# Conditioning products of a two-block kernel: four a group in groups 8 to 23 instead of two or three in each of 24

## The chip, the cores and the metric

One core of a Trainium2 chip runs the program. The metric is the device time of one execution in microseconds (us), lower is better. The engines are TensorE (PE; its weight loads are PEld), VectorE (DVE), ScalarE (ACT), GpSimd (POOL) and SyncE (SP). Each has its own instruction queue, and they wait for one another through semaphores.

## The reference

Two transformer-like blocks on a sequence of 512 with width 1024. The part that matters here is at the beginning of the first block:

```python
mod = (jax.nn.silu(c) @ w_ada[i] + b_ada[i])[:, None, :]
shift_m, scale_m, gate_m, shift_f, scale_f, gate_f = jnp.split(mod, N_MOD, axis=-1)
h = rmsnorm(x, norm_mix_w[i]) * (1.0 + scale_m) + shift_m
x = x + gate_m * hybrid_mixer(h, ...)      # begins with proj = h @ w_in, then a causal
                                           # convolution of width 4 over the xbc columns and silu
h = rmsnorm(x, norm_mlp_w[i]) * (1.0 + scale_f) + shift_f
```

`c` is one vector of 1024, `w_ada` is 1024 x 6144. Only `shift_m` and `scale_m`, a third of `mod`, are needed before the projection. The rest is needed much later: `gate_m` when the mixer's output is added, the others in the feed-forward part.

## The kernel before

**Linear layers.** All weight matrices are streamed in units of 8 x 128 rows by 128 columns (512 KB) through a ring of two buffers of each kind. SP loads a unit into `w_raw` (line 368) as soon as the split of the unit two earlier is done (semaphore `w_split`). ScalarE rounds it to `w_hi` (line 382, `split_hi`), after the load has landed and PE has finished the unit two earlier. VectorE forms `w_lo` = `w_raw` - `w_hi` (line 388, `split_lo`). PE then multiplies three times for each of the 8 k tiles, 24 products of 512 columns a unit (line 456, `products_of`).

**The first projection.** Before it, one unit computes the 32 step-size columns. Then come 24 groups of 128 columns of xbc, one unit each. For group g PE makes its 24 products; ScalarE takes the result out twice (lines 960 and 962) and makes `w_hi` of the unit two ahead. VectorE's queue has, in a Python loop that is unrolled and so sets its order: `split_lo` for the unit two ahead, the convolution `conv` (two instructions of line 1607 and one of line 1609), the group's `dt_steps`, and then a few products of `times_c`. ScalarE finishes with a silu (line 967). In `dt_steps` the step sizes are formed in groups 0, 2 and 3 (lines 1621 to 1635, ending in the semaphore `dt_done`), and `dt_decay` in groups 6 and 7. PE turns the step sizes into tokens between its groups 4 and 5 (line 1336), which waits for `dt_done`.

**Conditioning.** `mod` is formed in 12 blocks of 512 columns. For each, `times_c` on VectorE adds up 8 products of a row tile of `w_ada` with a column of silu(c): one of line 600 and seven of line 602, each waiting for the one before through `link`. Blocks 0 to 3 run before the projection. Blocks 4 to 11 run among the 24 groups of the projection, a block in three groups (2, 3 and 3 products). The tiles of `w_ada` are 2 MB each, in two buffers; POOL issues the load of block n (line 776) when block n - 2 is done. After PE's last group, `modulation` (line 1319) turns each block's sums into columns with tiny products; the last block's waits for its last product, VectorE adds the bias (lines 1651 and 1653, semaphore `mod_ready`), and PE waits for that before the chunked scan (line 1362 on).

Of the kernel before, what the change touches and what calls it, by code (L numbers as in the profile page):

```python
# [152 lines left out]
def two_block_program(nc, I, out):  # L153
    ctx = ExitStack()
    with ctx:
        sems = {}

        def sem(name):
            if name not in sems:
                sems[name] = ctx.enter_context(nc.semaphore(name))  # L160
            return sems[name]
# [223 lines left out]
        def split_lo(dve, l, t, par, j):  # L385
            slot, _ = slot_of(l, t, par, j, 2)
            dve.wait_ge(sem("w_hi_ready"), unit_of(l, t, par, j) + 3)
            dve.tensor_tensor(wlo[slot][:], wraw[slot][:], whi[slot][:].bitcast(F32), ALU.subtract).then_inc(  # L388
                sem("w_split"), 1)
# [204 lines left out]
        def times_c(dve, link, n, k0=0, k1=KD):  # L594

            u, slot, fill = (ADA_FIRST[n], n, 1) if n < 4 else (n, n % 2, n // 2)
            w, acc = wada[slot], ada_acc[u]
            if k0 == 0:
                dve.wait_ge(sem(f"ada_in{slot}"), 16 * fill)
                link(dve.tensor_scalar(acc[:], w[:, 0, :], small[:, 8:9], None, ALU.mult))  # L600
            for k in range(max(k0, 1), k1):
                ins = dve.scalar_tensor_tensor(acc[:], w[:, k, :], small[:, 8 + k:9 + k], acc[:], ALU.mult, ALU.add)  # L602
                if k < KD - 1:
                    link(ins)
                else:
                    ins.then_inc(sem("ada_acc"), 1)
# [64 lines left out]
        def lg_view(b, i):  # L671

            _, nq, nk, _ = TT[i]
            if nk <= 512:
                return two(PS[0:nq, b, 0:nk])
            return PS[0:nq, b:b + 2, 0:nk // 2]
# [14 lines left out]
        def probs_transposed(pe, i, p):  # L691

            _, nq, nk, ntile = TT[i]
            last = pe.transpose(PS[0:META, 1, 0:nq], p[0:nq, 0:META], ident[0:nq, 0:nq])
            for t in range(1, ntile):
                last = pe.transpose(PS[:, 0, (t - 1) * P:(t - 1) * P + nq], p[0:nq, META + (t - 1) * P:META + t * P],  # L696
                                    ident[0:nq, 0:nq])
            return last

        def values_product(pe, b, i, v, p):  # L700

            _, nq, _, ntile = TT[i]
            for t in range(ntile):
                rows = META if t == 0 else P
                last = pe.matmul(PS[:, b, 0:nq], v(t)[0:rows, :], p[0:rows, t, 0:nq], start=(t == 0),  # L705
                                 stop=(t == ntile - 1))
            return last
# [857 lines left out]
        def _(dve):  # L1565
            link = Link(dve, sem("dve_link"))
# [33 lines left out]
            def conv(g, t, par):  # L1600
                evacuated(dve, L["xbc"], t, par)

                dve.wait_ge(sem("conv_out"), t * 2 + par + 1)
                dve.wait_ge(sem("conv_pad"), 2)
                u, a = ub[par], ca[par]
                for k in (2, 1):
                    link(dve.scalar_tensor_tensor(a[:], u[:, 1 + k:1 + k + S], pcol("conv_w", k * NX + g), a[:],
                                                  ALU.mult, ALU.add))
                dve.scalar_tensor_tensor(a[:], u[:, 1:1 + S], pcol("conv_w", g), a[:], ALU.mult,
                                         ALU.add).then_inc(sem("conv_done"), 1)  # L1610
# [7 lines left out]
            def dt_steps(g):  # L1618
                if g == 0:
                    dve.wait_ge(sem("dt_act"), 3)  # L1620
                    dve.tensor_scalar(u, y, 1.0, None, ALU.add).then_inc(sem("dt_u"), 1)
                elif g == 2:
                    dve.wait_ge(sem("dt_act"), 4)
                    link(dve.tensor_scalar(u, u, 1.0, None, ALU.subtract))
                    link(dve.tensor_scalar(e, u, 0.0, None, ALU.is_equal))
                    link(dve.tensor_scalar(u, u, 1e-30, None, ALU.max))
                    link(dve.reciprocal(u, u))
                elif g == 3:
                    link(dve.tensor_tensor(l, l, y, ALU.mult))
                    link(dve.tensor_tensor(l, l, u, ALU.mult))  # L1630
                    link(dve.tensor_tensor(e, e, y, ALU.mult))
                    link(dve.tensor_tensor(l, l, e, ALU.add))
                    link(dve.tensor_scalar(v, v, 0.0, None, ALU.max))
                    link(dve.tensor_tensor(v, v, l, ALU.add))
                    dve.tensor_scalar(y, v, cst[:, 2:3], -1.0, ALU.mult, ALU.mult).then_inc(sem("dt_done"), 1)
                elif g == 6:
                    dve.wait_ge(sem("dt_tok"), 3)
                    dve.tensor_tensor(wdt[:], dtok[:, 3, :, :], dtok[:, 2, :, :], ALU.subtract).then_inc(
                        sem("dt_diff"), 1)
                elif g == 7:  # L1640
                    dve.wait_ge(sem("dt_tok"), 4)
                    link(dve.tensor_tensor(wdt[:], wdt[:], dtok[:, 0, :, :], ALU.mult))
            for g in range(NX):
                split_lo(dve, L["xbc"], g // 2, g % 2, 0)
                conv(g, g // 2, g % 2)
                dt_steps(g)
                n, third = 4 + g // 3, g % 3
                times_c(dve, link, n, *((0, 2), (2, 5), (5, 8))[third])

            dve.wait_ge(sem("ada_done"), 12)  # L1650
            link(dve.tensor_tensor(modc[:, 16:48], bank(7)[:, 16:48], PC[:, 16:48], ALU.add))
# [7 lines left out]
            for i in range(24):  # L1659
                if i < 16:  # L1660
                    g, c = STEPS[i]
# [329 lines left out]
```

## Time and profile before

| | us |
|---|---|
| median of 3 runs | 2889.18 |
| lowest, highest | 2887.94, 2900.04 |
| the profiled execution | 2890.59 |
| its span in the profile | 2888.6 |
| PE busy | 2583.7 (89%) |
| VectorE busy | 1539.1 (53%) |
| ScalarE busy | 1038.0 (36%) |

The busy times are of the profiled execution. The projection's 24 groups lie between about 54 and 213 us of its span, some 5% of it. Times within the span are counted from its start.

### The profile page before, as it was taken

The numbers are of one execution on the slowest core, as the hardware profiler recorded it, in microseconds if no ns is written. First come the engines' busy times: TensorE is split into PE (matmuls) and PEld (weight loads), VectorE is DVE, ScalarE is ACT, GpSimd is POOL, SyncE is SP. The second block draws the span as 40 slices with busy tenths as digits, with TensorE's granted clock in tenths as the row PEclk, the third lists the DMA queues.
The fourth block names the chain that finished last, engine by engine and source line by source line (L and its number), as shares of the span: only waits on it lengthen the run. The fifth ranks groups of instructions, "written<-read, shape, count | busy, mean of one in ns | idle before, by whom it ended". The sixth has DMA issues, their size and how long they took to land.

```text
span 2888.6 us, 41859 instructions
## 1 busy us (share of the span) xinstructions
PE 2583.7 (89%) x15307; PEld 2253.1 (78%) x15307; DVE 1539.1 (53%) x2178; ACT 1038.0 (36%) x1718; POOL 619.4 (21%) x522
## 2 busy tenths in 40 slices
PE   5898888998979999798666899999996996999998
PEld 4677766886858878697445899999995665899998
DVE  6884555424354233458555476642557556566631
ACT  5444443434333233233233333322433443333322
POOL 0000223610620102531112511222211002411110
PEclk8999999999989989888557999999996556999999
DMA  7551111332323333232000233323321000223322
GB/s 260 160 175 30 37 37 44 95 95 80 95 67 94 95 110 95 73 96 58 1 1 8 74 90 92 87 88 94 104 77 36 1 1 20 76 87 88 93 86 89
DMA packets 378054, 222.75 MB, mean 77 GB/s; under 512 B 9986, under 2 KB 368997, under 8 KB 377957
## 3 DMA queue, kind: packets, MB, share of 16 engines
q1 hardware_dynamic: 369189, 186.74, 22.9%
q0 software_dynamic: 8160, 32.53, 3.1%
q10 hardware_dynamic: 608, 2.16, 0.2%
q8 instruction: 64, 1.05, 0.2%
q14 instruction: 33, 0.27, 0.0%
HBM read 216.49 MB, written 4.78 MB: 77 GB/s over the span
## 4 chain that ended last, share of the span: by engine, by line
PE 76%; DVE 11%; issue 7%; ACT 3%; DMA 2%; POOL 2%; POOLq 0%; ACTq 0%; DVEq 0%; SPq 0%
PE PS L456 63%; PE PS L705 4%; PE PS L685 2%; DVE ada_acc L602 1%; DMA w_raw<-in_w_in_dram 1%; PE PS L687 1%; PE PS L1382 1%; DVE rstd_headB L1951 1%; PE PS L696 1%; ACT w_hi L382 1%; PE PS L1441 1%; DVE w_lo L388 1%; PE PS L1394 1%; DVE evac L1767 1%; DVE op_lo L558 1%
## 5 line engine op out<-in xcount | busy, mean ns | idle before, releaser
L388 DVE TENSOR_TENSOR w_lo<-w_raw,w_hi 128x1024 fp32r<-128x1024 f32 x360 | 494.8, 1374 | 863.1 <-ACT w_hi L382 862.7
L456 PE MATMUL PS<-op_hi,w_hi 128*128 128x264 f32 (+2 forms) x3048 | 806.5, 323 | 67.6 <-DVE op_lo L558 31.0
L456 PE MATMUL PS<-op_lo,w_hi 128*128 128x264 f32 (+2 forms) x3048 | 796.8, 320 | 0.0
L456 PE MATMUL PS<-op_hi,w_lo 128*128 128x264 f32 (+2 forms) x3048 | 793.6, 319 | 0.0
L456 PEld LDWEIGHTS PS<-op_hi,w_hi 128*128 128x128 f32 (+1 forms) x3048 | 511.7, 191 | 127.1 <-issue 39.2
L456 PEld LDWEIGHTS PS<-op_hi,w_lo 128*128 128x128 f32 (+1 forms) x3048 | 508.8, 191 | 38.4 <-issue 0.8
L456 PEld LDWEIGHTS PS<-op_lo,w_hi 128*128 128x128 f32 (+1 forms) x3048 | 509.5, 191 | 36.8 <-issue 0.9
L382 ACT ACTIVATE w_hi<-w_raw 128x1024 fp32r<-128x1024 f32 x360 | 379.1, 1053 | 219.0 <-PE PS L456 209.5
L456 PE MATMUL PS<-ff_hi,w_hi 128*128 128x264 f32 (+1 forms) x960 | 242.0, 312 | 0.0
L456 PE MATMUL PS<-ff_hi,w_lo 128*128 128x264 f32 (+1 forms) x960 | 242.0, 311 | 0.0
L456 PE MATMUL PS<-ff_lo,w_hi 128*128 128x264 f32 (+1 forms) x960 | 241.9, 311 | 0.0
L588 POOL TENSOR_TENSOR ff_u<-ff_u,rstd 128x528 f32<-128x528 f32 x88 | 100.4, 1142 | 429.5 <-ACT ff_u L1197 391.4
L1197 ACT ACTIVATE ff_u<-PS 128x528 f32<-128x528 f32 x88 | 54.0, 613 | 343.0 <-PE PS L456 313.1
L456 PEld LDWEIGHTS PS<-ff_lo,w_hi 128*128 128x128 f32 x960 | 157.0, 188 | 10.1
L456 PEld LDWEIGHTS PS<-ff_hi,w_hi 128*128 128x128 f32 x960 | 156.9, 188 | 10.0
L456 PEld LDWEIGHTS PS<-ff_hi,w_lo 128*128 128x128 f32 x960 | 156.7, 188 | 9.9
L645 POOL TENSOR_TENSOR evac<-resid,evac 128x528 f32<-128x528 f32 (+1 forms) x40 | 52.4, 1309 | 514.0 <-ACT evac L620 513.4
L705 PE MATMUL PS<-probsT,v_tokA 128*128 128x128 f32 (+2 forms) x240 | 60.1, 387 | 76.1 <-ACT probsT L1173 75.6
L705 PEld LDWEIGHTS PS<-probsT,v_tokA 128*128 128x128 f32 (+1 forms) x240 | 45.2, 257 | 103.1 <-ACT probsT L1173 93.7
L643 POOL TENSOR_TENSOR resid<-resid,evac 128x512 f32 (+1 forms) x16 | 20.9, 1306 | 301.6 <-ACT evac L620 301.6
L705 PEld LDWEIGHTS PS<-probsTB,v_tokB 128*128 128x128 f32 (+1 forms) x240 | 53.2, 301 | 35.2 <-issue 26.2
L1743 DVE TENSOR_TENSOR norm_v<-evac 128x512 f32<-128x512 f32 x32 | 22.1, 692 | 107.3 <-ACT evac L1084 107.3
(343 smaller groups left out, 3548.7 us busy)
## 6 DMA issues: line engine op xcount, KB each, us to landing
w_raw<-in_w_up_dram SPq DMA_DIRECT2D x120, 512.0 KB, 3.9
w_raw<-in_w_in_dram SPq DMA_DIRECT2D x64, 512.0 KB, 4.0
w_raw<-in_w_down_dram SPq DMA_DIRECT2D x64, 512.0 KB, 3.9
w_ada<-in_w_ada_dram POOLq DMA_DIRECT2D x12, 2048.0 KB, 10.2
w_raw<-in_w_branch_ssd_dram SPq DMA_DIRECT2D x16, 512.0 KB, 3.9
w_raw<-in_w_in_a_dram SPq DMA_DIRECT2D x16, 512.0 KB, 3.8
w_raw<-in_w_kv_b_dram SPq DMA_DIRECT2D x16, 512.0 KB, 3.8
w_raw<-in_w_down_dram SPq DMA_DIRECT2D x16, 384.0 KB, 3.4
```

Source lines behind the costliest of these rows:

```text
L382: act.activation(whi[slot][:], wraw[slot][:], ACT.Copy).then_inc(sem("w_hi_ready"), 1)
L388: dve.tensor_tensor(wlo[slot][:], wraw[slot][:], whi[slot][:].bitcast(F32), ALU.subtract).then_inc(sem("w_split"), 1)
L456: last = pe.matmul(a[0:l.cols, h, 0:cn], w[slot][:, k, 0:l.cols], x[:, kk, c0:c0 + cn], start=(j == 0 and k == 0 and w is whi and x is l.h ...
L558: dve.scalar_tensor_tensor(lo[:, k, :], R[:, k, :], gain(k), hi[:, k, :].bitcast(F32), ALU.mult, ALU.subtract).then_inc(sem("norm_ready"), 1)
L588: pool.tensor_tensor(x, x, rs[0:L[name].cols, :], ALU.mult).then_inc(sem("scaled"), 1)
L602: ins = dve.scalar_tensor_tensor(acc[:], w[:, k, :], small[:, 8 + k:9 + k], acc[:], ALU.mult, ALU.add)
L645: link(pool.tensor_tensor(e, r, e, ALU.add))
L685: return pe.matmul(PS[0:nq, b, 0:nk], q[:, q0:q0 + nq], k[:, 0:nk], start=True, stop=True)
L687: last = pe.matmul(PS[0:nq, b + a, 0:nk // 2], q[:, q0:q0 + nq], k[:, a * nk // 2:(a + 1) * nk // 2], start=True, stop=True)
L696: last = pe.transpose(PS[:, 0, (t - 1) * P:(t - 1) * P + nq], p[0:nq, META + (t - 1) * P:META + t * P], ident[0:nq, 0:nq])
L705: last = pe.matmul(PS[:, b, 0:nq], v(t)[0:rows, :], p[0:rows, t, 0:nq], start=(t == 0), stop=(t == ntile - 1))
L1197: act.activation(halves(uu[par][:, 2:2 + T]), acc_view(l, par), ACT.Copy).then_inc(sem("evacuated"), 1)
```

## The change

The 64 products of blocks 4 to 11 no longer stand in all 24 groups. Groups 0 to 7 have none. Groups 8 to 23 have four each, a block in two groups.

```diff
                 split_lo(dve, L["xbc"], g // 2, g % 2, 0)
                 conv(g, g // 2, g % 2)
                 dt_steps(g)
-                n, third = 4 + g // 3, g % 3
-                times_c(dve, link, n, *((0, 2), (2, 5), (5, 8))[third])
+                if g >= 8:
+
+                    n, half = 4 + (g - 8) // 2, (g - 8) % 2
+                    times_c(dve, link, n, 4 * half, 4 * half + 4)
```

Only VectorE's order differs. In its queue, at the step sizes of group 2 and the beginning of group 3 (`dtT` holds the step sizes, `ada_acc` the sums of a block, `w_ada` its tile), the difference reads:

```order
 L1626 TENSOR_SCALAR dtT<-dtT 32x512
 L1627 RECIPROCAL dtT<-dtT 32x512
-L602 SCALAR_TENSOR_TENSOR ada_acc_88<-w_ada_80,small,ada_acc_88 128x512 x3
 L388 TENSOR_TENSOR w_lo_56<-w_raw_52,w_hi_54 128x1024
 L1607 SCALAR_TENSOR_TENSOR conv_acc_99<-conv_in_97,param_cols,conv_acc_99 128x512 x2
```

The last three products of block 4 are gone from between the reciprocal and the split of group 3. Further on in VectorE's queue, groups 8 and 9 stood so before (the first three products close block 6, the last two open block 7):

```order
L388 TENSOR_TENSOR w_lo_57<-w_raw_53,w_hi_55 128x1024
L1607 SCALAR_TENSOR_TENSOR conv_acc_98<-conv_in_96,param_cols,conv_acc_98 128x512 x2
L1609 SCALAR_TENSOR_TENSOR conv_acc_98<-conv_in_96,param_cols,conv_acc_98 128x512
L602 SCALAR_TENSOR_TENSOR ada_acc_90<-w_ada_80,small,ada_acc_90 128x512 x3
L388 TENSOR_TENSOR w_lo_56<-w_raw_52,w_hi_54 128x1024
L1607 SCALAR_TENSOR_TENSOR conv_acc_99<-conv_in_97,param_cols,conv_acc_99 128x512 x2
L1609 SCALAR_TENSOR_TENSOR conv_acc_99<-conv_in_97,param_cols,conv_acc_99 128x512
L600 TENSOR_SCALAR ada_acc_91<-w_ada_81,small 128x512
L602 SCALAR_TENSOR_TENSOR ada_acc_91<-w_ada_81,small,ada_acc_91 128x512
```

In the changed kernel the same two groups read:

```order
L388 TENSOR_TENSOR w_lo_57<-w_raw_53,w_hi_55 128x1024
L1607 SCALAR_TENSOR_TENSOR conv_acc_98<-conv_in_96,param_cols,conv_acc_98 128x512 x2
L1609 SCALAR_TENSOR_TENSOR conv_acc_98<-conv_in_96,param_cols,conv_acc_98 128x512
L600 TENSOR_SCALAR ada_acc_88<-w_ada_80,small 128x512
L602 SCALAR_TENSOR_TENSOR ada_acc_88<-w_ada_80,small,ada_acc_88 128x512 x3
L388 TENSOR_TENSOR w_lo_56<-w_raw_52,w_hi_54 128x1024
L1607 SCALAR_TENSOR_TENSOR conv_acc_99<-conv_in_97,param_cols,conv_acc_99 128x512 x2
L1609 SCALAR_TENSOR_TENSOR conv_acc_99<-conv_in_97,param_cols,conv_acc_99 128x512
L602 SCALAR_TENSOR_TENSOR ada_acc_88<-w_ada_80,small,ada_acc_88 128x512 x4
```

Two groups now hold eight products, a whole block, and block 4 opens here instead of in group 0. The queues of PE, ScalarE, POOL and SP hold the same instructions in the same order as before; the loads of `w_ada` for blocks 6 to 11 still wait for the blocks two earlier, so they go out later.

## Rows read from the trace of the kernel before

**Rows 1.** Windows, the time of VectorE's groups 8 to 23.

```profile
core 0: us, PE busy (x) PEld busy (x) DVE busy (x) ACT busy (x) POOL busy (x), PEclk, DMA share, GB/s
120.60:212.70 92.10, 88.07 (x401) 70.91 (x400) 83.43 (x108) 42.83 (x62) 3.53 (x4) 0.98 0.60 182
```

**Rows 2.** Timeline of VectorE, from group 9: start us, us, what.

```profile
126.28 1.22 DVE L388 TENSOR_TENSOR w_lo<-w_raw,w_hi 128x1024 fp32r<-128x1024 f32 x1
...
129.65 0.48 DVE L600 TENSOR_SCALAR ada_acc<-w_ada,small 128x512 f32<-128x512 f32 x1
130.17 0.75 DVE L602 SCALAR_TENSOR_TENSOR ada_acc<-w_ada,small,ada_acc 128x512 f32<-128x512 f32 x1
130.96 1.23 DVE L388 TENSOR_TENSOR w_lo<-w_raw,w_hi 128x1024 fp32r<-128x1024 f32 x1
...
138.08 1.23 DVE L388 TENSOR_TENSOR w_lo<-w_raw,w_hi 128x1024 fp32r<-128x1024 f32 x1 [1.42 <-ACT w_hi L382]
```

**Rows 3.** Waits of VectorE, 60 to 120, then 120.6 to 212.7: us, times, longest.

```profile
DVE w_lo L388 <- ACT w_hi L382: 11.9, 6, 5.0
...
DVE w_lo L388 <- ACT w_hi L382: 6.3, 4, 1.9
```

**Rows 4.** The chain that ended last: start us, us, what.

```profile
92.46 7.54 PE PS L456 x24
100.44 5.57 PE PS L456 x24
...
127.68 9.21 DMA w_raw<-in_w_in_dram
136.92 1.07 ACT w_hi L382
...
145.10 9.70 DMA w_raw<-in_w_in_dram
```

**Rows 5.** Timeline of VectorE, groups 2 and 3.

```profile
81.26 2.33 DVE L602 SCALAR_TENSOR_TENSOR ada_acc<-w_ada,small,ada_acc 128x512 f32<-128x512 f32 x3
83.50 1.22 DVE L388 TENSOR_TENSOR w_lo<-w_raw,w_hi 128x1024 fp32r<-128x1024 f32 x1
...
90.88 0.47 DVE L1635 TENSOR_SCALAR dtT<-dtT,dt_consts 32x512 f32<-32x512 f32 x1
```

**Rows 6.** The tile `w_ada`, its twelve loads.

```profile
DMA to landing us min/median/max: 8.8/10.2/29.6
```

**Rows 7.** Timeline of PE around the step sizes.

```profile
80.88 0.39 PE L456 MATMUL PS<-op_hi,w_lo 128*128 128x512 f32 x1
91.41 1.05 PE L1336 MATMUL PS<-mats,dtT 32*128 32x32 f32 x8 [10.14 <-DVE dtT L1635]
```

**Rows 8.** Timeline of VectorE, the start of group 8 and the last products.

```profile
118.30 2.33 DVE L602 SCALAR_TENSOR_TENSOR ada_acc<-w_ada,small,ada_acc 128x512 f32<-128x512 f32 x3
120.66 1.23 DVE L388 TENSOR_TENSOR w_lo<-w_raw,w_hi 128x1024 fp32r<-128x1024 f32 x1
...
210.33 2.32 DVE L602 SCALAR_TENSOR_TENSOR ada_acc<-w_ada,small,ada_acc 128x512 f32<-128x512 f32 x3
```

**Rows 9.** Timeline of ScalarE, `w_hi` before group 8's split.

```profile
119.46 1.06 ACT L382 ACTIVATE w_hi<-w_raw 128x1024 fp32r<-128x1024 f32 x1
```

**Rows 10.** Windows in the scan; the columns are those of rows 1.

```profile
244.00:250.00 6.00, 3.86 (x18) 3.56 (x19) 3.30 (x5) 2.48 (x3) 1.04 (x1) 0.72 0.21 62
286.00:292.00 6.00, 4.73 (x33) 3.85 (x33) 2.94 (x4) 2.25 (x4) 0.00 (x0) 1.00 0.10 23
```

**Rows 11.** Timeline of PE, the stalls in these two windows.

```profile
246.14 0.85 PE L1373 MATMUL PS<-mats,y_tok 128*128 128x128 f32 x4 [2.91 <-DVE y_tok L1694]
291.59 0.66 PE L1373 MATMUL PS<-mats,y_tok 128*128 128x128 f32 x4 [1.27 <-DVE y_tok L1696]
```

**Rows 12.** Timeline of PE, the last column and the scan's start.

```profile
212.71 1.87 PE L1319 MATMUL PS<-mats,ada_acc 128*128 128x1 f32 x8 [2.23 <-DVE ada_acc L602]
215.06 0.79 PE L1362 MATMUL PS<-xbc 128*128 128x128 f32 x2 [0.48 <-DVE aff_cols L1653]
```

## The prediction, made before the changed kernel ran

> **What bounds the kernel now.** Over the whole span TensorE (PE) is the busiest engine by far, but such an average says little about an edit to one stage. So I looked first at the windows of the first block's projection, about 54 to 213 us. From 120.6 to 212.7 us, the time in which VectorE runs its groups 8 to 23, PE is busy for 88.07 of 92.10 us, VectorE for 83.43, and the clock is 0.98 of full [rows 1]. Two engines are nearly full side by side. The reader is to see that VectorE has only about 8 us of room left in these 92, before a single instruction is moved there.
>
> The timeline of VectorE shows what a group is made of [rows 2]. Group 9 starts with its split at 126.28 and comes to its first product of conditioning block 7 at 129.65: split and convolution take 3.37 us, start to start. The block's first product takes 0.52 us (129.65 to 130.17), the next one 0.79 (130.17 to 130.96); the last product of a block, which nothing on VectorE waits for, is followed after 0.67, since three products that close a block last 2.24 in all (81.26 to 83.50) [rows 5]. A block of eight so costs 0.52 + 6 x 0.79 + 0.67 = 5.93 us, and three groups with one block 3 x 3.37 + 5.93 = 16.04 us.
>
> PE's 24 products of a group take 5.57 us in the chain that ended last [rows 4], so three groups take it 16.7 us. Work on VectorE would fit below that. It does not quite: the split at 138.08 comes late, and the waits of VectorE say for what: `w_hi` of ScalarE, 6.3 us in 4 times [rows 3]. The chain goes one step further [rows 4]: a split ends at 127.5, the weight load that it frees takes 9.21 us, ScalarE's copy 1.07, and only then can the split of 138.08 begin. In the next block the load takes 9.70. These are the loads that meet a 2 MB load of `w_ada`, which goes out when a block closes, here just before the split of 126.28.
>
> Ahead of that lies one bigger stall. PE stops after 80.88 and its transposes start at 91.41 [rows 7], because they wait for the step sizes (line 1635), at 90.88 on VectorE [rows 5]. Three products of block 4 stand in front of that, from 81.26 to 83.50.
>
> **The change, part by part.**
>
> *Groups 0 to 7 lose their products.* 21 instructions go: blocks 4 and 5 whole and the first five of block 6. In groups 0, 1 and 3 to 7 nobody waits for them: VectorE idles 11.9 us in 6 times for `w_hi` between 60 and 120 us [rows 3], and the few products do not bring a split behind PE's need. I take 0 for those; they could at most bring what group 8 gains, below. In group 2 they cost 2.24 us right in the path to line 1635. PE then starts at 91.41 - 2.24 = 89.17: **-2.24 us**. The clock was slow in this gap: the 24 products behind it take 7.54 instead of 5.57 us [rows 4], 1.97 us more. A gap of some 8 us instead of 10 will still see it fall, since a gap of 2.91 did: the window with it has a granted clock of 0.72 [rows 10, 11]. So I leave the 1.97 as they are; bounds are 1.97 less and about 2 more.
>
> *The start of group 8.* Its split starts at 120.66 [rows 8]. Two things end just before: the three products of group 7 (118.30 + 2.36 = 120.66) and ScalarE's `w_hi`, at 119.46 + 1.06 = 120.52 [rows 9]. The first is now gone; the second moves with PE by 2.24. Group 8 starts at about 118.4, so the gain here is the same 2.24 and no more.
>
> *Groups 8 to 23 take all 64 products.* They had 43. The 21 that come are 2 x 5.93 + (0.52 + 4 x 0.79) = **+15.5 us** of VectorE. Now a pair of groups costs 2 x 3.37 + 5.93 = 12.67 us, one group 6.33, against PE's 5.57. VectorE becomes the bound, PE will wait about 0.76 us in each group for `w_lo`. Queued behind the products on VectorE are the next split and the convolution, and for the split both PE and the next weight load wait.
>
> *The waits for late weight loads go away.* From the end of a split to the start of the split two groups later there were 0.17 us to the issue, 9.21 to 9.70 to the landing, 1.07 for `w_hi` and 0.1: with the split's 1.23 a round of 11.8 to 12.3 us. The round of VectorE now lasts 12.67, so a landing may take 10.1 us before anybody waits. Six `w_ada` loads meet a weight load in the stage, one every second group. I take the 6.3 us of waits as hidden: **-6.3 us**. What covers them is VectorE's own work; if that cover is too thin, every microsecond by which a landing passes 10.1 comes back six times. Bounds: 0 and 6 x 1.9 = 11.4 us. I stay near 0, because the second weight load of a pair is now spread over a longer round, and the rows of the four met loads lie 0.4 to 0.9 us under the limit. The `w_ada` loads themselves land in 10.2 us in the median [rows 6], and have a round and a group's head, 12.67 + 3.37 = 16 us, until their first product.
>
> *The end of the stage.* Before, the last product ends at 210.33 + 2.32 = 212.65 [rows 8]; PE forms the last column at 212.71 and begins the scan at 215.06 [rows 12]. Product, column, `mod_cols`: this chain stays as it is, and PE has long finished its own group 23 in both kernels. So the whole of what follows moves by what the last product moves.
>
> Sum: -2.24 + 15.5 - 6.3 = **+7.0 us**. The same by the rounds: 8 x 12.67 = 101.4 us from 118.4 ends at 219.8, 7.1 later than 212.65. The profiled execution took 2890.59 us, of which the span is 2888.6; the median of the runs is 2889.18, 1.4 us lower. So profiled about 2897.6, and as a median **2896.2 us**, 0.24% slower. 0.5%, some 14 us, is about what a measurement of this kernel can tell from no change; this is half of it.
>
> **The rivals.**
>
> *A: the clock falls in the new rhythm (over 0.5% slower).* PE gets a stall in every group where it had one in three. Against it: the window 286 to 292 has a stall of 1.27 us before `y_tok` and keeps a clock of 1.00, and 4.73 us busy of 6 [rows 10, 11]; the new stall is 0.76. For it: the 2.91 us stall next door brings the clock down. The price: at the half clock a group takes 2 x 5.57 = 11.1 us, 4.8 more than VectorE's 6.33. Two such groups take +7.0 over 14.4 us; from there on this rival decides. All sixteen would give +84 us, 2973. Chance 0.07.
> The Trainium skill speaks for this rival (TensorE: Matmul & The Clock Gate, A second HAM failure mode: psum-queue depth-cycling): in a kernel with 512-column products the engine idled briefly between groups often enough that the clock swung between its two levels. By that rule the sum would be that of rival A; by the rows of 286 to 292 it stays +7.0, and I go by the rows.
>
> *B: loads set the pace.* Loads of `w_ada` come every 12.67 us instead of every 16 to 18, and six instead of four meet a weight load. If each costs 1 us, +13 us, 2902; if each 1.9, the longest wait of before, +18.4, 2907.6. Against it: the margin above. Chance 0.10, a fifth of it past 0.5%.
>
> *C: the clock returns sooner after the shorter gap.* -1.97: +5.0, 2894.2. It only shades the forecast; chance 0.05, and as much for the opposite, held in the forecast's own range.
>
> *D: the products fit beside PE.* If a product took 0.55 us instead of 0.79, four of them and the 3.37 would fit into PE's 5.57 and PE stay the bound: -2.24 - 6.3 = -8.5, 2880.7, still within 0.5%. Against it: the products take the same in the quiet of group 2 (2.24 for three that close a block), and in group 7 (2.36 for three linked ones) as in the busy stretch [rows 2, 5, 8]. Chance 0.02.
>
> **How the numbers follow.** Forecast 0.76 (its own range 2893 to 2900), A 0.07, B 0.10, C 0.05, D 0.02. The range reaches from 2890, between D and C, to 2905, which takes in B up to 1.5 us a load. Slower by over 0.5%: 0.07 + 0.02 of B = 0.09; faster by over 0.5% is left with 0.01; within it 0.90.
>
> **What would show it.** Right: line 1635 ends about 2.2 us earlier and PE resumes near 89.2; VectorE from about 118.4 to 219.7 without a gap over 0.5 us, with splits 6.2 to 6.4 us apart; PE short stalls of some 0.8 us released by `w_lo`; clock 1.00 up to 205; the scan starts near 222. Wrong: waits of VectorE for `w_hi` in the stage (B), a granted clock under 1 between 125 and 205 (A), splits 5.6 apart (D), or a later part of the program that takes more or less time than before, which this working takes as unchanged.

## The result, and the profile after

| | before | changed kernel |
|---|---|---|
| median of 20 runs, us | 2891.62 | 2899.12 |
| lowest, highest | 2885.20, 2901.98 | 2893.20, 2910.24 |
| the profiled execution | 2890.59 | 2910.24 |
| its span | 2888.6 | 2908.2 |

The ratio is 1.0028, with a 95% interval of 1.0017 to 1.0038: the changed kernel is 0.28% slower, 8 us (the two medians differ by 7.5). The forecast was 0.24%, with a chance of 0.90 for a change within 0.5%. The forecast in microseconds, 2896.2, lies 2.9 below the measured median; 2.4 of that is its starting point, 2889.18 in three runs and 2891.62 in twenty. The profiled execution is the slowest of the 20; 12 of its 20 us come from later parts of the program and are taken up below.

VectorE's timeline (start us, us, what) shows the early gain and the new round.

```profile
81.51 1.23 DVE L388 TENSOR_TENSOR w_lo<-w_raw,w_hi 128x1024 fp32r<-128x1024 f32 x1
...
88.90 0.47 DVE L1635 TENSOR_SCALAR dtT<-dtT,dt_consts 32x512 f32<-32x512 f32 x1
...
119.08 1.23 DVE L388 TENSOR_TENSOR w_lo<-w_raw,w_hi 128x1024 fp32r<-128x1024 f32 x1 [2.42 <-ACT w_hi L382]
...
125.33 1.23 DVE L388 TENSOR_TENSOR w_lo<-w_raw,w_hi 128x1024 fp32r<-128x1024 f32 x1
...
131.74 1.22 DVE L388 TENSOR_TENSOR w_lo<-w_raw,w_hi 128x1024 fp32r<-128x1024 f32 x1
...
137.99 1.23 DVE L388 TENSOR_TENSOR w_lo<-w_raw,w_hi 128x1024 fp32r<-128x1024 f32 x1
...
217.27 3.11 DVE L602 SCALAR_TENSOR_TENSOR ada_acc<-w_ada,small,ada_acc 128x512 f32<-128x512 f32 x4
```

The split of group 3 follows the reciprocal at once, and line 1635 starts at 88.90, where it was 90.88 [rows 5]. From group 8 on the splits are 6.25 and 6.41 us apart by turns: 125.33 - 119.08, 131.74 - 125.33, 137.99 - 131.74. The last product ends at 217.27 + 3.11 = 220.38, against 212.65 [rows 8]. The waits from 118 to 220 us (us in total, times, longest) show who waits now.

```profile
PE PS L456 <- DVE w_lo L388: 5.8, 12, 0.6
...
DVE w_lo L388 <- ACT w_hi L382: 2.4, 1, 2.4
...
ACT w_hi L382 <- DMA w_raw<-in_w_in_dram: 12.8, 6, 2.4
```

VectorE waits once, for its group 8. The 6.3 us in four waits of [rows 3] are gone. ScalarE waits for a late weight load six times (four times and 8.2 us before), and it reaches nobody: VectorE is still busy with its products when `w_hi` comes. PE waits for `w_lo` in short pieces. The windows (columns as in rows 1) give the shares and the clock.

```profile
119.10:220.40 101.30, 92.36 (x401) 72.60 (x399) 98.16 (x128) 43.50 (x62) 5.30 (x6) 0.96 0.68 207
...
136.00:142.00 6.00, 5.59 (x25) 4.21 (x24) 5.82 (x8) 1.27 (x2) 0.00 (x0) 1.00 1.07 360
154.00:160.00 6.00, 5.44 (x24) 4.12 (x23) 5.82 (x9) 3.65 (x5) 0.88 (x1) 1.00 0.54 114
```

VectorE is busy for 98.16 of 101.3 us, PE for 92.36. Inside the stage the clock stays at its upper level, 2.4 GHz (1.00), though PE is busy for only 5.4 to 5.6 of 6 us. The 0.96 of the whole stretch comes from its end: the clock falls at about 211 us, when PE is already behind its last group and at the column products. Last, PE's timeline and the chain at the two ends.

```profile
89.43 1.06 PE L1336 MATMUL PS<-mats,dtT 32*128 32x32 f32 x8 [7.84 <-DVE dtT L1635]
...
220.43 1.86 PE L1319 MATMUL PS<-mats,ada_acc 128*128 128x1 f32 x8 [3.15 <-DVE ada_acc L602]
222.78 0.79 PE L1362 MATMUL PS<-xbc 128*128 128x128 f32 x2 [0.48 <-DVE aff_cols L1655]
```

```profile
90.49 7.97 PE PS L456 x24
98.90 5.57 PE PS L456 x24
```

PE resumes at 89.43 instead of 91.41 [rows 7], the 24 products behind that take 7.97 instead of 7.54 us [rows 4], and the scan starts at 222.78 instead of 215.06 [rows 12].

### The profile page after: what moved, and what is told of

It is laid out like the page before. It is cut to its first block, busy times and chain, and to the rows that moved or that the text cites. A ratio compares the mean times of both kernels' runs of the same rounds, so it can differ in the third digit from the quotient of the medians.

```text
span 2908.2 us, 41853 instructions
## 1 busy us (share of the span) xinstructions
PE 2609.1 (90%) x15307; PEld 2271.2 (78%) x15307; DVE 1538.3 (53%) x2178; ACT 1039.5 (36%) x1718; POOL 618.9 (21%) x522
## 4 chain that ended last, share of the span: by engine, by line
PE 76%; DVE 11%; issue 7%; ACT 3%; POOL 2%; DMA 1%; POOLq 0%; ACTq 0%; DVEq 0%; SPq 0%
PE PS L456 63%; PE PS L705 4%; PE PS L685 2%; DVE ada_acc L602 2%; PE PS L687 1%; PE PS L1382 1%; DVE rstd_headB L1953 1%; PE PS L696 1%; ACT w_hi L382 1%; DVE conv_acc L1607 1%; DVE w_lo L388 1%; PE PS L1441 1%; DVE evac L1769 1%; DVE op_lo L558 1%; DMA w_ada<-in_w_ada_dram 1%
## 5 line engine op out<-in xcount | busy, mean ns | idle before, releaser
L456 PEld LDWEIGHTS PS<-ff_lo,w_hi 128*128 128x128 f32 x960 | 157.0, 188 | 10.1
```

The source lines that it names most:

```text
L456: last = pe.matmul(a[0:l.cols, h, 0:cn], w[slot][:, k, 0:l.cols], x[:, kk, c0:c0 + cn], start=(j == 0 and k == 0 and w is whi and x is l.h ...
```

## The experiments

"Scan start" is the first instruction of the scan on PE (line 1362). It is read in one profile of each kernel, and repeats within 1 us: 215.1 and 216.0 for the kernel before, 222.8 and 222.5 for the changed one. Except for the last two versions there is only one timed run of each experiment, and single runs of one kernel lie up to 17 us apart, so the stage is judged by its profile and not by the time of the run.

### What repeats: both kernels once more

No edit.

> The changed kernel unchanged, to see what of it repeats. Its first profile had the scan start (first instruction of line 1362) at 222.8 us, 7.7 later than before, but a span 19.6 longer. Theory (VectorE's queue sets the stage, the rest of the program only scatters with the clock): scan start again 222.3 to 223.3, while the distance from there to the end may differ by up to some 12 us from the first profile's 2685.4. Rival (the change also lengthens a later part): scan start the same and the distance to the end again near 2685, against 2673.5 before.

> The kernel before, unchanged, as the other half of the same question. Theory: scan start 214.6 to 215.6; the distance from there to the end anywhere between 2672 and 2686. Rival: the distance again near 2673.5, clearly under that of the changed kernel.

Scan start 222.5 and 216.0: in the two pairs of profiles the stage costs 6.5 to 7.7 us. From there to the first copy into `out_tok`, the last stage of the program, it is 2673.2 us in `after_again` and 2672.0 in `before_again`. In the first profiles it was 2677.4 and 2665.5. The large difference of the first pair, 12 us, does not repeat. But a small part of it does. The first head sum of the second block stands at 1271.9 and 1272.7 in the kernel before, at 1281.1 and 1280.9 in the changed one, so 8.2 to 9.2 us apart, each repeating within 1 us. Between scan start and there, the changed kernel first gains 2 us and then loses 4. One such place is the `pool_w` layer, where PE waits for ScalarE between short groups. PE's timeline, before and then changed:

```profile
698.57 0.47 PE L456 MATMUL PS<-op_hi,w_hi 128*128 128x512 f32 x1 [1.96 <-ACT evac L1067]
701.08 0.47 PE L456 MATMUL PS<-op_hi,w_hi 128*128 128x512 f32 x1 [0.87 <-ACT evac L1067]
```

```profile
705.83 0.47 PE L456 MATMUL PS<-op_hi,w_hi 128*128 128x512 f32 x1 [1.95 <-ACT evac L1067]
712.06 0.47 PE L456 MATMUL PS<-op_hi,w_hi 128*128 128x512 f32 x1 [1.48 <-ACT evac L1067]
```

The windows with them, before and changed:

```profile
692.00:712.00 20.00, 13.03 (x52) 8.99 (x51) 11.80 (x13) 14.48 (x20) 1.27 (x1) 1.00 0.13 39
```

```profile
697.50:717.50 20.00, 14.50 (x53) 10.17 (x53) 11.15 (x12) 13.11 (x19) 1.28 (x1) 0.91 0.11 33
```

The same stall, 1.96 and 1.95 us, is followed by a clock that holds in one kernel and falls in the other, in both profiles of each. From the last product of the branch layer to the last of the next one with `pool_hi` it takes 66.8 us before and 69.2 after. And there is one part that really scatters: the second attention takes from its first to its last instruction of line 685 163.2 us in the first profile of the kernel before and 169.9 in the second. The windows of the two:

```profile
2212.00:2375.00 163.00, 155.86 (x503) 105.85 (x504) 88.08 (x387) 68.66 (x255) 0.00 (x0) 0.54 0.00 1
```

```profile
2212.70:2383.00 170.30, 165.10 (x504) 111.48 (x504) 88.78 (x389) 69.24 (x256) 0.00 (x0) 0.50 0.00 1
```

The changed kernel takes 169.9 in both. So of the 12 us in the first pair 6.7 are this attention, about 4 lie between the first head sum and this attention in the first profile of the changed kernel alone (944.2 us, 940.0 to 940.1 in the other three), and 1.5 are the part that repeats.

### One part alone: group 2

```diff
                 n, third = 4 + g // 3, g % 3
-                times_c(dve, link, n, *((0, 2), (2, 5), (5, 8))[third])
+                if g == 3:
+                    times_c(dve, link, 4, 5, 8)
+                if g != 2:
+                    times_c(dve, link, n, *((0, 2), (2, 5), (5, 8))[third])
```

> The kernel before with one part alone: the three products of block 4 that stand between the reciprocal of group 2 and the split of group 3 are issued behind line 1635 in group 3; all else as before. Theory: line 1635 ends 2.24 us earlier, PE resumes near 89.2, and with the later groups as before the scan starts near 212.8. Rival (the gain is lost to the clock or to the five products that now stand ahead of the split of group 4): scan start 214.5 or later.

PE resumes at 89.35 and the scan starts at 214.00, 1.1 and 2.0 us before the two profiles of the kernel before, between the 212.8 of the theory and the 214.5 of its rival. So the early part is a gain by itself, of about 1.5 us rather than 2.24. Windows of half a microsecond show when the clock returns, in `before`, `before_again` and this run:

```profile
96.00:96.50 0.50, 0.50 (x3) 0.45 (x2) 0.50 (x2) 0.00 (x0) 0.00 (x0) 0.72 1.06 312
```

```profile
97.00:97.50 0.50, 0.50 (x3) 0.42 (x3) 0.46 (x2) 0.00 (x0) 0.00 (x0) 1.00 0.33 96
```

```profile
95.00:95.50 0.50, 0.50 (x3) 0.37 (x3) 0.46 (x2) 0.00 (x0) 0.00 (x0) 0.83 1.03 401
```

PE resumes 2 us earlier, and the clock returns 1.1 and 1.8 us earlier. The 24 products take 7.97 us here, 7.54 and 7.91 before. Of the 1.2 us missing against the first profile, 0.2 are lost at PE's resuming, 0.4 with the clock and the rest in the later groups, where VectorE waits 6.9 instead of 6.3 us for `w_hi`. The two profiles of the kernel before differ by 0.4 us in the same 24 products, so this is near the limit of what a single profile shows.

### The loads away: in both kernels

```diff
-            for n in range(12):
+            for n in range(6):
...
-                dve.wait_ge(sem(f"ada_in{slot}"), 16 * fill)
+                dve.wait_ge(sem(f"ada_in{slot}"), 16 * min(fill, 2))
```

> The changed kernel without the loads of w_ada for blocks 6 to 11; those blocks are formed from the tiles of blocks 4 and 5, so the modulation's values are wrong and only its timing is read. Theory (in the changed kernel VectorE's own work covers the slow weight loads): nothing changes, groups stay 6.33 us apart, scan start 222.5 to 223.0. Rival B (loads set the pace): splits move closer and the scan starts at 220 or earlier.

> The kernel before without the loads of w_ada for blocks 6 to 11 (those blocks use the tiles of blocks 4 and 5, so the modulation's values are wrong and only the timing is read). Theory (in the kernel before, VectorE's 6.3 us of waits come from weight loads that meet a w_ada load, and are what its shorter groups have as reserve): the four waits of 1.4 to 2.0 us between 120 and 212 us are gone, PE runs its groups 5.57 us apart, the scan starts near 210, 5 to 6 us earlier than the 215.1 and 216.0 of before, while the same edit in the changed kernel moved nothing. Rival (the waits come from somewhere else in the order of VectorE or ScalarE): scan start 214 or later.

In the changed kernel nothing moves: the scan starts at 223.24, splits are still 6.40 and 6.25 us apart (151.09, 157.49, 163.74), PE waits for `w_lo` as before. These are its waits from 119 to 212 us:

```profile
PE PS L456 <- DVE w_lo L388: 5.9, 12, 0.6
DVE w_lo L388 <- ACT w_hi L382: 2.4, 1, 2.4
```

ScalarE's waits for a weight load, 13.2 us in `after_again`, are gone, and it made no difference. This decides against rival B. In the kernel before, the same edit takes VectorE's waits from 6.3 to 2.7 us. The long ones are gone, and four of 0.5 to 0.8 us stand there instead, at the pace of PE, which is busy for all of the 91.40 us from 120.6 to 212.0. It ends its last group at 201.5 instead of 203.5. The scan starts at 213.1, 2 to 3 us earlier, and not the 5 to 6 that I expected; it lies between the theory's 210 and the rival's 214. PE's timeline says why:

```profile
201.48 11.15 PE L1319 MATMUL PS<-mats,ada_acc 128*128 128x1 f32 x64
213.11 0.79 PE L1362 MATMUL PS<-xbc 128*128 128x128 f32 x2 [0.48 <-DVE aff_cols L1653]
```

The 64 column products stand in one piece behind PE's last group and take 11.15 us, where I had reckoned 8 from 56 of them in 7. The stage has a second end: the piece ends at 212.63, 2.5 us behind the last product.

### The price of a product: three and five a group

```diff
-                    times_c(dve, link, n, 4 * half, 4 * half + 4)
+                    times_c(dve, link, n, 5 * half, 5 * half + 3)
```

> The changed kernel with three products instead of four in each of groups 8 to 23, so products 3 and 4 of blocks 4 to 11 are left out and the modulation is incomplete. VectorE's group then holds 3.37 + 2.2 = 5.55 us against PE's 5.57. Theory (VectorE's work is the bound at four a group; under PE's 5.57 it no longer covers the loads): the stage does not get the whole 16 x 0.79 = 12.6 us back, because the round of two groups, 11.1, is shorter than the 11.8 to 12.3 that a weight load beside a w_ada load needs; six waits of about 0.9 us return and the scan starts near 215. Rival (products cost their full length and loads nothing): scan start near 210.

```diff
+                    if half:
+                        times_c(dve, link, n, 3, 4)
                     times_c(dve, link, n, 4 * half, 4 * half + 4)
+                    if not half:
+                        times_c(dve, link, n, 3, 4)
```

> The changed kernel with five products instead of four in each of groups 8 to 23: product 3 of each block is added two more times, which changes the modulation's values. Theory (VectorE is the bound, each product on it costs its 0.79 us in full): groups 7.12 us apart, scan start 16 x 0.785 = 12.6 us later than the changed kernel, near 235; clock still 1.00 in the stage up to 220. Rival A (the clock gives way to the stalls, now 1.5 us in each group): granted clock under 1 in some windows between 125 and 215 and more than 13 us.

With five the scan starts at 234.66, 11.9 to 12.2 us later than with four (12.6 expected); splits are 7.19 and 7.03 us apart and PE waits 14.8 us for `w_lo` from 119 to 212 us. Counted from the start of group 8 (118.33 here, 119.08 and 118.76 with four) it takes 116.3 instead of 103.7 us, and the difference is the whole 12.6. With three it starts at 212.38, 10.1 to 10.4 earlier, and lies between what the theory (215) and its rival (210) gave. VectorE's waits for `w_hi` are back, three of 0.9, 0.6 and 0.7 us beside the one at group 8, where I had expected six of 0.9. So a product costs its 0.79 us in full at four and five, and at three a small part is taken by the loads again. The windows of the kernel with five:

```profile
160.00:180.00 20.00, 16.09 (x68) 12.12 (x67) 19.36 (x27) 8.54 (x12) 1.77 (x2) 1.00 0.62 198
180.00:200.00 20.00, 16.26 (x68) 12.25 (x67) 19.36 (x26) 6.96 (x10) 0.88 (x1) 1.00 0.79 255
```

PE stands still for up to 1.4 us in every group and is busy for 80%, and its clock is 1.00. Rival A does not occur even at twice the stall that it was forecast for, 0.76.

### The same four, from group 4 on

```diff
-                if g >= 8:
-                    n, half = 4 + (g - 8) // 2, (g - 8) % 2
+                if 4 <= g < 20:
+                    n, half = 4 + (g - 4) // 2, (g - 4) % 2
```

> The changed kernel with its four products a group in groups 4 to 19 instead of 8 to 23; nothing is left out. Theory (the loss comes from VectorE being full in groups 8 to 23 while groups 5 to 8 hold 15.5 us of waits for w_hi): the products of groups 4 to 8 go into those waits, the last four groups have none, the chain over the last product is replaced by PE's own end at about 208 plus its 64 column products of 8 us, and the scan starts near 216.7, 6 us earlier than in the changed kernel. Rival (VectorE's order does not matter, only that a group holds four): scan start near 222.5.

The scan starts at 220.50, only 2.0 to 2.3 us earlier than in the changed kernel. PE ends its groups at 208.6, as expected, and then:

```profile
208.59 11.43 PE L1319 MATMUL PS<-mats,ada_acc 128*128 128x1 f32 x64
220.50 0.80 PE L1362 MATMUL PS<-xbc 128*128 128x128 f32 x2 [0.48 <-DVE aff_cols L1654]
```

The direction was right, and the size was wrong by 3.8 us, 3.4 of them the time that the column products take beyond 8. By its number alone the scan start lies nearer to the rival's 222.5 than to the 216.7 of the theory; PE's end at 208.6 is what speaks for the theory. Once the last product is early, the column products are what the scan waits for.

### Versions that use it

The products go where VectorE waits: 2, 3, 0, 3 and 8 in groups 0 to 4, then 3, 3, 2 by turns up to group 22 (`SPREAD` holds for each group the pieces of its blocks; `COUNTS` is the same list of counts; the lines that fill the two are left out here).

```diff
-                n, third = 4 + g // 3, g % 3
-                times_c(dve, link, n, *((0, 2), (2, 5), (5, 8))[third])
+                for n, k0, k1 in SPREAD[g]:
+                    times_c(dve, link, n, k0, k1)
```

> The kernel before with its 64 products spread by VectorE's waits: 2, 3, 0, 3 and 8 in groups 0 to 4, then 3, 3 and 2 by turns in groups 5 to 22 and none in group 23; nothing is left out. Theory (neither VectorE nor the last product is the bound any more, but the 64 column products behind PE's group 23 then run in one piece at the half clock): PE resumes near 89.2 and ends its groups near 201, the 64 column products take 11.2 to 11.5 us as in the two kernels where they ran in one piece, and the scan starts near 213. Rival (the end of the stage follows the last product alone): last product near 206 and scan start near 209.

The second version also moves the columns among PE's groups:

```diff
-            products(pe, L["xbc"], None, 6, dt_steps)
-            for n in range(4, 12):
+            formed = [4]
+
+            def columns(g):
+                dt_steps(g)
+                done, n = sum(COUNTS[:max(0, g - 1)]), formed[0]
+                if n < 12 and (done >= 8 * (n - 3) or g == NX - 1):
+                    modulation(n)
+                    formed[0] += 1
...
+            products(pe, L["xbc"], None, NX, columns)
+            for n in range(formed[0], 12):
                 modulation(n)
```

> The same spread of products, and PE forms the columns of each block between its groups, two groups behind the last product of the block, instead of all behind group 23. Theory (what is left of the stage's end is the piece of 64 small products at the half clock; among the groups they run at the full clock, 1 us a block): scan start near 209 to 210, 5 to 6 us before the kernel before and 12 to 13 before the changed kernel; median of the runs 2883 to 2889 against about 2891.5 before. Rival (the small products cost PE's groups more than they save at the end): scan start 213 or later, no gain.

And the third computes the step sizes first in group 3:

```diff
+                if g == 3:
+                    dt_steps(g)
                 split_lo(dve, L["xbc"], g // 2, g % 2, 0)
                 conv(g, g // 2, g % 2)
-                dt_steps(g)
+                if g != 3:
+                    dt_steps(g)
```

> The same again, and in group 3 VectorE computes the step sizes (lines 1629 to 1635) before the split and the convolution of that group. Theory (PE's stall between its groups 4 and 5 is VectorE's queue, 3.4 us of it the split and the convolution): PE resumes at about 85.8 instead of 89.2, the scan starts about 3 us earlier again, near 206 to 207; median 2880 to 2887. Rival (the split for PE's group 5 now comes late, or the clock gives the gain back): scan start near 209.

| | PE resumes | scan start | median, us | ratio to before, 95% |
|---|---|---|---|---|
| before | 91.4, 91.3 | 215.1, 216.0 | 2891.62 | |
| changed | 89.4, 89.1 | 222.8, 222.5 | 2899.12 | 1.0028 (1.0017 to 1.0038) |
| spread_only | 89.6 | 211.0 | one run: 2886.15 | |
| spread_and_columns | 89.0 | 211.1 | 2887.24 | 0.9989 (0.9976 to 1.0002) |
| steps_first | 86.0 | 210.3 | 2886.72 | 0.9978 (0.9966 to 0.9990) |

The last two were timed in 12 and 11 runs, beside 23 runs of the kernel before with a median of 2892.21 us; one of the 23 took 5649.78 us and is not in the ratios. `steps_first` is faster than both kernels, by 0.22% against before; `spread_and_columns` by 0.11%, with an interval that just takes in no difference. Their medians differ by 0.5 us, which does not tell the two apart. The medians lie in the forecast ranges, the scan starts do not: 211.0 is between the 213 and 209 of theory and rival, 211.1 is later than the 209 to 210 of the second theory, and 210.3 is what the rival of the third named (209) rather than its theory (206 to 207).

The spread alone brings the scan 4 to 5 us forward. Its last product ends at 201.4 and is waited for by nobody; the end is PE's last group at 198.9 and 64 column products in 11.67 us. Forming the columns among the groups makes them cheap but does not move the scan: seven blocks of 0.79 us each now stand in PE's path, and it ends its groups at 204.3 instead of 198.9. PE's timeline of `spread_and_columns`:

```profile
104.22 0.95 PE L1319 MATMUL PS<-mats,ada_acc 128*128 128x1 f32 x8
121.80 0.95 PE L1319 MATMUL PS<-mats,ada_acc 128*128 128x1 f32 x8
206.30 1.87 PE L1319 MATMUL PS<-mats,ada_acc 128*128 128x1 f32 x8 [2.04 <-DVE ada_acc L602]
...
211.07 0.77 PE L1371 MATMUL PS<-xbc 128*128 128x128 f32 x2 [2.90 <-ACT xbc L967]
```

Eight of them take 0.95 us there instead of 1.4 to 1.5. But now the third end of the stage shows: the last convolution and its silu, which ends at 210.81, 6.5 us behind PE's last group. In `steps_first` PE resumes 3.0 us earlier than in `spread_and_columns`, and 0.8 is left of it at the scan. The rest goes in group 7, where ScalarE waits 3 us for a weight load. ScalarE's timeline of `steps_first`, and the chain that ended last:

```profile
112.80 1.06 ACT L382 ACTIVATE w_hi<-w_raw 128x1024 fp32r<-128x1024 f32 x1 [2.97 <-DMA w_raw<-in_w_in_dram]
```

```profile
100.71 1.23 DVE w_lo L388
102.11 10.67 DMA w_raw<-in_w_in_dram
112.80 1.07 ACT w_hi L382
```

The load takes 10.67 us beside a load of `w_ada` issued at 101.1 on POOL, and it was freed by the split at 100.71. That split has not moved (100.38 in `spread_and_columns`): up to it the chain runs along VectorE's queue without a wait, with the eight products that these versions put into group 4 in front of it. So two things give the gain back, the full queue and then the slow load, as rival B had it for the changed kernel. How much each takes was not tested.

## Why the prediction was right

- **The bound.** "VectorE becomes the bound" and "one group 6.33": the splits are 6.25 and 6.41 us apart, and VectorE is busy for 97% of the time. Three and five products a group move the scan by -10 and +12 us, so the time follows VectorE's work. PE's waits for `w_lo` are shorter than the 0.76 us of the forecast, 5.8 us in 12, the longest 0.6: the first product behind each wait itself takes 0.50 us instead of 0.39.
- **+15.5 us of products.** From the start of group 8 to the last product it takes 101.3 us, reckoned 101.4, in the kernel before 92.0.
- **-6.3 us of waits.** All four are gone. `after_no_reload` shows that the loads do not matter any more at all, `before_no_reload` that without them 2.7 of the 6.3 us are left in the kernel before, at PE's own pace of 5.57, and that PE gains 2 us by it.
- **-2.24 us early.** The step that was mis-sized, by a little. PE resumes 2.0 to 2.2 us earlier, of which the clock takes back up to 0.4: 7.97 and 8.01 us for the 24 products after, 7.54 and 7.91 before. That lies within the bounds that were given. In the first pair of profiles group 8 starts 1.58 us earlier (119.08 against 120.66) and not 2.24, and this explains most of what the pair has beyond the sum, 7.7 against 7.0 us.
- **The end of the stage.** It is the chain over the last product, as said: product at 220.38, column at 220.43, scan at 222.78. In the kernel before, the column products of all blocks are as near to being the end: in `before_again` they run in one piece from 203.95, for 11.58 us, and the scan starts at 216.0, where the last product, at 213.09, would have allowed an earlier start. That is why the second pair shows 6.5 us and not the 7.0 by which its last products differ (220.06 and 213.09). "PE has long finished its own group 23" was true of the group in both kernels, but its column products, which the working left out, were not finished with it.
- **What follows the stage** was taken as unchanged. It is not quite: the clock falls at other stalls when the program is shifted. At the first head sum of the second block this makes 1 to 2 us more than at the scan start. The timed 8 us agree with the sum of both; that the phase is the cause was not tested.
- **The rivals.** A fell with `five_a_group`, B with `after_no_reload`, D with the splits' distance. C did not occur: the clock returned with PE, 1.0 to 2.0 us earlier, and the 24 products took no less than before. For A the working had counted a stall of PE in one group of three before; the trace has three in the 16 groups.

## What to carry to other kernels

An engine with idle time in a stage's average may have none where you put the work. Count what it does in one round, set that against the round of the engine that is fed, and keep the surplus ahead of, not inside, the stretch where both are full. When two engines' rounds are nearly equal, look for the next end of the stage before moving the first: in the kernel before three ends (last silu 211.1, last product 212.65, last column 214.6) lie within 4 us, so each repair gave less than its own length. A wait that vanishes because the waiting engine got slower is not a gain, it is cover.

## What the runs showed of the hardware

- Small products of one column run 0.95 us for eight among PE's large groups, and 11.2 to 11.7 us for 64 in one piece behind them (1.4 to 1.5 for eight; 1.86 at a granted clock of 0.50 throughout). The clock is what makes the difference. Windows of `before_again`, whose piece begins at 203.95:

```profile
204.00:206.00 2.00, 2.00 (x21) 2.00 (x19) 1.93 (x4) 1.70 (x3) 0.00 (x0) 1.00 0.79 203
207.00:215.00 8.00, 8.00 (x39) 8.00 (x39) 5.92 (x8) 0.66 (x2) 0.00 (x0) 0.50 0.23 66
```

  It falls to 0.50, 1.2 GHz, some 2.3 us into the piece, and stays there while the profile shows PE busy for 8.00 of 8 us. `four_from_group4`, `spread_only` and `before_no_reload` are alike (2.2 to 2.7 us into it). In the first profile of the kernel before it falls only after 5.4 us, and 56 of the products take 6.99 us, against 9.09 in the changed kernel. The Trainium skill (TensorE: Matmul & The Clock Gate, What's actually happening) has the clock follow how busy the engine was; here the busy share of the profile does not show the fall coming.
- A stall of up to 1.4 us in every group of 7.1 us, with PE busy for 80%, leaves the clock at 1.00 for 80 us (`five_a_group`, 120 to 200). A single stall of 1.95 to 1.96 us lets it fall in one kernel and not in the other, in two profiles of each. The length of a stall alone does not decide.
- The same part of the program, the second attention, takes 163.2 or 169.9 us in two executions of one kernel, with a granted clock of 0.54 and 0.50. That is 6.7 of the 12 us by which the first pair of profiles differs behind the scan start. Why the clock was higher in one of them was not tested.
